# Depthwise convolution taps split anew between four engines

## The reference

```python
def conformer_conv_module(h, w_in, dw, norm_g, norm_b, w_out):
    u = h @ w_in                                  # 2048 -> 4096
    a, g = jnp.split(u, 2, axis=-1)
    u = a * jax.nn.sigmoid(g)
    u = causal_depthwise_conv(u, dw)              # 31 taps per channel
    u = jax.nn.silu(layer_norm(u, norm_g, norm_b))
    return u @ w_out

def causal_depthwise_conv(h, w):                  # out[t] = sum_k w[k] * h[t - 30 + k]
    ...
```

## Time and profile before

| | us |
|---|---|
| median of three runs (2061.01 to 2061.51) | 2061.35 |
| span of the profiled execution | 2059.6 |
| median less span | 1.75 |
| TensorE busy | 2039.1 |
| VectorE busy | 1451.8 |
| ScalarE busy | 981.0 |
| GpSimd busy | 197.6 |

### The profile page before, as it was taken

One profiled execution on the slowest core, in us unless ns is written; L12 is line 12 of the kernel. 1 busy time (PEld: TensorE's weight loads), 2 busy tenths in 40 slices (PEclk: granted clock), 3 DMA queues, 4 the chain that ended last, 5 costly groups with the idle time before them and its releaser, 6 DMA issues.

```text
span 2059.6 us, 36156 instructions
## 1 busy us (share of the span) xinstructions
PE 2039.1 (99%) x11524; PEld 1760.0 (85%) x11524; DVE 1451.8 (70%) x2280; ACT 981.0 (48%) x1295; POOL 197.6 (10%) x123
## 2 busy tenths in 40 slices
PE   9999999999999999999999999999999999999997
PEld 7877888888888888888899988888888888888886
DVE  5477687777677676454699998777777777774545
ACT  4455454444444444343555555544444444444432
POOL 1000000000000000000199920000000000000001
PEclk9999999999999999999999999999999999999999
DMA  7544546656656666555465646565665665676553
GB/s 254 190 129 134 190 150 198 194 177 191 197 183 188 199 203 219 193 193 193 134 189 174 176 154 199 158 198 176 201 193 173 199 193 178 189 256 221 194 192 132
DMA packets 346329, 383.81 MB, mean 186 GB/s; under 512 B 23151, under 2 KB 269471, under 8 KB 345201
## 3 DMA queue, kind: packets, MB, share of 16 engines
q1 hardware_dynamic: 344320, 373.12, 57.4%
q0 software_dynamic: 1360, 7.34, 1.0%
q10 hardware_dynamic: 576, 2.36, 0.3%
HBM read 380.24 MB, written 2.10 MB: 186 GB/s over the span
## 4 chain that ended last, share of the span: by engine, by line
PE 95%; DVE 3%; ACT 1%; issue 0%; DMA 0%; SPq 0%; POOL 0%; POOLq 0%; DVEq 0%; ACTq 0%
PE ps L352 31%; PE ps L348 16%; PE ps L250 11%; PE ps L251 11%; PE ps L252 11%; PE ps L1675 8%; PE ps L265 1%; PE ps L267 1%; PE ps L266 1%; DVE w_lo L218 1%; PE ps L1579 0%; PE ps L1590 0%; PE ps L1606 0%; DVE stats L595 0%; DVE x L589 0%
## 5 line engine op out<-in xcount | busy, mean ns | idle before, releaser
L218 DVE TENSOR_TENSOR w_lo<-raw,w_hi 128x1024 fp32r<-128x1024 f32 x641 | 781.6, 1224 | 489.1 <-ACT w_hi L213 482.4
L213 ACT ACTIVATE w_hi<-raw 128x1024 fp32r<-128x1024 f32 x704 | 743.7, 1059 | 684.6 <-PE ps L252 309.2
L352 PE MATMUL ps<-xT,w_hi 128*128 128x512 f32 x2800 | 960.7, 394 | 0.0
L348 PE MATMUL ps<-xT,w_lo 128*128 128x256 f32 x2800 | 749.7, 277 | 0.0
L352 PEld LDWEIGHTS ps<-xT,w_hi 128*128 128x128 f32 x2800 | 513.2, 188 | 107.2
L348 PEld LDWEIGHTS ps<-xT,w_lo 128*128 128x128 f32 x2800 | 525.9, 188 | 14.9
L250 PE MATMUL ps<-w_hi,hT 128*128 128x512 f32 x828 | 324.2, 392 | 0.2 <-DVE hT L1461 0.2
L252 PE MATMUL ps<-w_hi,hT 128*128 128x512 f32 x828 | 322.4, 389 | 0.0
L251 PE MATMUL ps<-w_lo,hT 128*128 128x512 f32 x828 | 322.3, 389 | 0.0
L1675 PE MATMUL ps<-xT,w_hi 128*128 128x256 f32 x1024 | 191.7, 287 | 1.1 <-DVE xT L709 0.6
L250 PEld LDWEIGHTS ps<-w_hi,hT 128*128 128x128 f32 x828 | 155.4, 188 | 35.2 <-issue 1.4
(11 more groups left out here) (191 smaller groups left out, 1433.7 us busy)
## 6 DMA issues: line engine op xcount, KB each, us to landing
raw<-in_ffn_w_up_dram SPq DMA_DIRECT2D x704, 256.0 KB, 3.2
raw<-in_ffn_w_down_dram SPq DMA_DIRECT2D x352, 256.0 KB, 3.3
raw<-in_conv_w_in_dram SPq DMA_DIRECT2D x128, 256.0 KB, 3.1
raw<-in_attn_wq_dram SPq DMA_DIRECT2D x64, 256.0 KB, 3.3
raw<-in_attn_wo_dram SPq DMA_DIRECT2D x64, 256.0 KB, 3.3
raw<-in_conv_w_out_dram SPq DMA_DIRECT2D x64, 256.0 KB, 3.3
raw<-in_attn_wk_dram SPq DMA_DIRECT2D x16, 256.0 KB, 5.3
raw<-in_attn_wv_dram SPq DMA_DIRECT2D x16, 256.0 KB, 4.2
```

Of the source, the lines that this page charges most:

```text
L213: nc.scalar.activation(w_hi[:, slot, :], raw[:, slot, :], ACT.Copy).then_inc(hi_ready, 1)
L218: v.tensor_tensor(w_lo[:, slot, :], raw[:, slot, :], w_hi[:, slot, :].bitcast(F32), ALU.subtract).then_inc(lo_ready, 1)
L348: nc.tensor.matmul(ps[:, bank, 0:T], wl, xT[:, k, 0:T], start=False, stop=False, skip_group_check=True)
L352: mm = nc.tensor.matmul(ps[:, bank, :], wh, xT[:, k, :], start=(k == 0), stop=(k == KD - 1), skip_group_check=True)
```

## The change

- Tiles 0 to 13: TensorE has no tap, VectorE 27, ScalarE 4 products. GpSimd adds the products in pairs, in one instruction of 2 x 256 columns, and `added` holds two sums. VectorE's first two taps read them as the value to add to (in tile 0 they are added behind tap 18), so an add of VectorE's and the add of TensorE's tap go.
- The gate product of tile `u + 1`, with the statistics behind it, comes behind the 18th tap of tile `u` instead of behind the tile.
- Tile 14: 17 taps on VectorE, 8 products, 6 taps on TensorE (4 between the halves of unit 15, 2 behind it). Tile 15: 9, 8 and 14. What GpSimd adds of the later products goes to `rest`, which VectorE adds (`tile_rest`).
- ScalarE makes tile 15's products between the third and the fourth rounding of `w_out`'s first turn.
- GpSimd makes the low parts of `w_out`'s first turn. The two broadcasts have a bank each, and VectorE's first step waits for them one by one.

```diff
-LAST_PE_TAPS = 16
-MORE_PE_TAPS = 4
-PE_TAPS = 1
-ACT_TAPS = 4
-DVE_TAPS = CW - PE_TAPS - ACT_TAPS
-TILE_STEPS = DVE_TAPS + 1
+ACT_TAPS = [4] * (D // P - 2) + [8, 8]
+PE_TAPS = [0] * (D // P - 2) + [6, 14]
+MID_PE_TAPS = 4
+DVE_TAPS = [CW - a - p for a, p in zip(ACT_TAPS, PE_TAPS)]
+BEFORE_GLU = 18
...
-        diag = at("diag", [P, LAST_PE_TAPS, P], F32, HT_AT)
-        tile_diag = at("tile_diag", [P, 2, MORE_PE_TAPS, P], F32, HT_AT + 12288)
-        products = at("products", [P, ACT_TAPS, T], F32, HT_AT + 16384)
-        added = at("added", [P, T], F32, HT_AT + 16384 + ACT_TAPS * T * 4)
+        diag = at("diag", [P, sum(PE_TAPS), P], F32, HT_AT)
+        products = at("products", [P, max(ACT_TAPS), T], F32, HT_AT + 16384)
+        added = at("added", [P, 2, T], F32, HT_AT + 24576)
+        rest = at("rest", [P, T], F32, HT_AT + 26624)
...
+        def tap_diag(a, i):
+            u = KD - 2 if i < PE_TAPS[KD - 2] else KD - 1
+            j = CW - PE_TAPS[u] + (i if u < KD - 1 else i - PE_TAPS[KD - 2])
+            nc.scalar.activation(diag[:, i], ident[:], ACT.Copy, scale=conv_taps[:, u, j:j + 1]
+                                 ).then_inc(diag_ready, 1)
+        def steps_before(u):
+            return sum(DVE_TAPS[:u]) + (u > 0)
+        def added_used(u):
+            return BEFORE_GLU + 1 if u == 0 else steps_before(u) + 2
...
             if u > 0:
-                a.wait_ge(products_added, 2 * u)
-            for i in range(ACT_TAPS):
-                j = DVE_TAPS + i
+                a.wait_ge(taps, added_used(u - 1))
+            if u == KD - 1:
+                a.wait_ge(products_added, KD + 1)
+            for i in range(ACT_TAPS[u]):
+                j = DVE_TAPS[u] + i
                 nc.scalar.activation(products[:, i], glu[:, u % 2, j:j + T], ACT.Copy,
                                      scale=conv_taps[:, u, j:j + 1]).then_inc(products_made, 1)
...
-                v.wait_ge(pe_taps_done, u - 1)
-                v.wait_ge(products_made, ACT_TAPS * (u - 1))
+                v.wait_ge(products_made, sum(ACT_TAPS[:u - 1]))
...
-        def tile_taps(v, u, n, with_products=False):
...
+        def tile_taps(v, u, between=None):
...
+            o, n, count, last = conv_out[:, u], DVE_TAPS[u], steps_before(u), [0, 0]
+            halves = [ps[:, 4, i * T:(i + 1) * T] for i in range(2)]
             v.wait_ge(glu_done, u + 1)
             if u > 0:
                 v.wait_ge(part_sum, u)
+            if 0 < u < KD - 1:
+                v.wait_ge(products_added, u + 1)
...
+                part, i = halves[j % 2], j % 2
+                tap, src = conv_taps[:, u, j:j + 1], glu[:, u % 2, j:j + T]
+                if u == 0 and j == BEFORE_GLU:
+                    v.wait_ge(products_added, 1)
+                    v.wait_ge(taps, count)
+                    nc.vector.tensor_tensor(ps[:, 4, :], ps[:, 4, :], added[:].rearrange("p a t -> p (a t)"), ALU.add
+                                            ).then_inc(taps, 1)
+                    count += 1
+                    last = [count, count]
+                if between is not None and j == BEFORE_GLU:
+                    between()
+                if j < 2 and u in (0, KD - 1):
                     step = nc.vector.tensor_scalar(part, src, tap, None, ALU.mult)
                 else:
-                    v.wait_ge(taps, base + j - 1)
-                    step = nc.vector.scalar_tensor_tensor(out=o if j == n - 1 else part, in0=src, scalar=tap, in1=part,
+                    if j >= 2:
+                        v.wait_ge(taps, last[i])
+                    step = nc.vector.scalar_tensor_tensor(out=o if j == n - 1 else part, in0=src, scalar=tap,
+                                                          in1=added[:, j] if j < 2 else part,
                                                           op0=ALU.mult, op1=ALU.add)
                 step.then_inc(taps, 1)
-            v.wait_ge(taps, base + n)
-            other = ps[:, 4, n % 2 * T:(n % 2 + 1) * T]
-            nc.vector.tensor_tensor(o, o, other, ALU.add).then_inc(part_sum, 1)
+                count += 1
+                last[i] = count
+            v.wait_ge(taps, count)
+            nc.vector.tensor_tensor(o, o, halves[n % 2], ALU.add).then_inc(part_sum, 1)
+        def tile_rest(v, u):
+            o = conv_out[:, u]
+            v.wait_ge(products_added, KD + 1 if u == KD - 2 else KD + 5)
+            v.wait_ge(part_sum, u + 1)
+            nc.vector.tensor_tensor(o, o, rest[:], ALU.add).then_inc(rest_added, 1)
         def tile_sum(v, u):
             o = conv_out[:, u]
-            v.wait_ge(part_sum, u + 1)
-            v.wait_ge(pe_taps_done, u + 1)
+            v.wait_ge(rest_added, u - KD + 3)
+            v.wait_ge(pe_taps_done, u - KD + 3)
             nc.vector.tensor_tensor(o, o, ps[:, 5 if u < KD - 1 else 1, 0:T], ALU.add).then_inc(tile_done, 1)
...
             with pool.Fori(first + 1, first + KD - 1) as turn:
                 w_in_lows(turn)
-                pool.wait_ge(products_made, turn * ACT_TAPS + (-ACT_TAPS * first))
-                nc.gpsimd.tensor_tensor(products[:, 0:2], products[:, 0:2], products[:, 2:4], ALU.add
-                                        ).then_inc(products_added, 1)
-                pool.wait_ge(products_added, turn * 2 + (-2 * first - 1))
-                nc.gpsimd.tensor_tensor(added[:], products[:, 0], products[:, 1], ALU.add
+                pool.wait_ge(products_made, turn * 4 + (-4 * first))
+                nc.gpsimd.tensor_tensor(added[:], products[:, 0:2], products[:, 2:4], ALU.add
                                         ).then_inc(products_added, 1)
             w_in_lows(first + KD - 1)
+            made = 4 * (KD - 2)
+            pool.wait_ge(products_made, made + 4)
+            nc.gpsimd.tensor_tensor(added[:], products[:, 0:2], products[:, 2:4], ALU.add).then_inc(products_added, 1)
+            pool.wait_ge(products_made, made + 8)
+            nc.gpsimd.tensor_tensor(products[:, 4:6], products[:, 4:6], products[:, 6:8], ALU.add
+                                    ).then_inc(products_added, 1)
+            pool.wait_ge(products_added, KD)
+            nc.gpsimd.tensor_tensor(rest[:], products[:, 4], products[:, 5], ALU.add).then_inc(products_added, 1)
+            w_in_lows(first + KD, (0, 1))
+            pool.wait_ge(products_made, made + 12)
+            nc.gpsimd.tensor_tensor(added[:], products[:, 0:2], products[:, 2:4], ALU.add).then_inc(products_added, 1)
+            pool.wait_ge(products_made, made + 16)
+            nc.gpsimd.tensor_tensor(products[:, 4:6], products[:, 4:6], products[:, 6:8], ALU.add
+                                    ).then_inc(products_added, 1)
+            pool.wait_ge(products_added, KD + 3)
+            nc.gpsimd.tensor_tensor(added[:], added[:], products[:, 4:6], ALU.add).then_inc(products_added, 1)
+            pool.wait_ge(products_added, KD + 4)
+            pool.wait_ge(rest_added, 1)
+            nc.gpsimd.tensor_tensor(rest[:], added[:, 0], added[:, 1], ALU.add).then_inc(products_added, 1)
+            w_in_lows(first + KD, (2, 3))
...
-                tile_diags(a, u)
                 tile_sigmoid(a, u)
-                for i in range(2 * u, min(2 * u + 2, LAST_PE_TAPS)):
-                    j = CW - LAST_PE_TAPS + i
-                    nc.scalar.activation(diag[:, i], ident[:], ACT.Copy, scale=conv_taps[:, KD - 1, j:j + 1]
-                                         ).then_inc(diag_ready, 1)
+                for i in range(2 * u, min(2 * u + 2, sum(PE_TAPS))):
+                    tap_diag(a, i)
                 if u < KD - 1:
                     splits(a, TURN["w_in"] + u + 1, [RING - 1])
+                    tile_products(a, u)
                 if u < KD - 2:
...
-            splits(a, TURN["w_out"])
+            splits(a, TURN["w_out"], range(RING - 1))
+            tile_products(a, KD - 1)
+            splits(a, TURN["w_out"], [RING - 1])
...
-            for u in range(KD - 1):
+            def next_glu(u):
                 tile_glu(v, u)
                 if u % 4 == 2 and u > 2:
                     for tok in range(TT):
                         c_stat(2 * (u // 4 - 1) + tok)
-                if u < KD - 2:
-                    tile_taps(v, u, TILE_STEPS, with_products=True)
-                else:
-                    tile_taps(v, u, CW - PE_TAPS - MORE_PE_TAPS)
-                if u < KD - 2:
-                    tile_sum(v, u)
+            tile_glu(v, 0)
+            for u in range(KD - 2):
+                tile_taps(v, u, lambda: next_glu(u + 1))
+            tile_taps(v, KD - 2)
             tile_glu(v, KD - 1)
+            tile_rest(v, KD - 2)
             tile_sum(v, KD - 2)
-            tile_taps(v, KD - 1, CW - LAST_PE_TAPS)
+            tile_taps(v, KD - 1)
             c_stat(6)
             c_stat(7)
+            tile_rest(v, KD - 1)
             tile_sum(v, KD - 1)
...
-            take_lo(v, TURN["w_out"], 0)
-            v.wait_ge(c_bcast, 1)
...
```

(50 more changed lines are left out.)

46 lines of the change are left out of this document (5 added, 41 removed).

## The result

| | before | after |
|---|---|---|
| median (us), four runs of each | 2061.18 (2060.84 to 2061.51) | 2105.57 (2105.47 to 2105.78) |
| ratio, 95% interval | | 1.0215 (1.0203 to 1.0228) |
| span of the profiled execution | 2059.6 | 2103.8 |
| TensorE busy | 2039.1 | 2047.1 |

The account below looks back on a forecast made before the run. TensorE bounded the kernel, with VectorE next and by a hair the bound after the change; 3.6 (last gate product) + 1.3 (tail) + 0.4 + 0.5 (into w_out), about 5.85 us, off 2061.35 gave 2055.5 us, range 2053.0 to 2063.0.

Parts of the forecast that it names:

- The unknown price: Taps 0 and 1 and the rest sum read two SBUF tensors beside GpSimd: taken as nothing, at most 2.4 us per wait.
- rival 2: In tiles 1 to 13 first taps wait for whole GpSimd instructions, 1.2 to 3.6 us a tile: 2071 to 2102; chance 0.16.
- TensorE's stream: Convolution stage: tiles 0 to 13 lose their TensorE tap, 6.05 us; unit 15's value half ends at 1202.87 instead of 1207.62.
- VectorE's start of tile 1: VectorE waits 2.7 us for GpSimd's sums, then runs free from 1044.6.
- VectorE's tile: A tile without statistics takes VectorE 11.46 us instead of 11.89; last gate product at 1204.3, 3.6 us earlier.
- rival 1: VectorE stays later than worked out through longer steps, stretched taps or late sums: 2059.7 at 0.3 us a tile; chance 0.16.
- The tail: From the last gate product to the last sum: 7.8 us instead of 9.1, 1.3 less.
- Into w_out: The first step's add waits only for the second broadcast, 1221.3 instead of 1221.73: 0.4 us; fewer hT waits: 0.5.
- the hT waits: In w_out TensorE waits twice for VectorE's hT; three fewer VectorE low parts save 0.5 us, bounds 0.2 and 1.0.
- The rest sum: VectorE's add of `rest` at the stage's end reads two SBUF tensors beside GpSimd; no extra time was reckoned.

Follow-up runs that it names:

- experiment 6: Kernel before, with the second tap of tiles 0 to 13 writing its product to SBUF instead of PSUM: 2065.78 us, ratio 1.0023.
- experiment 8: Changed kernel with sums copied to PSUM for the taps, w_out's last two low parts held until the last rest sum, tile 1 begun as tile 0: 2059.51 us.
- experiment 9: As experiment 8, but w_out's last two low parts are VectorE's again, as in the kernel before: 2056.12 us, ratio 0.9976.
- experiment 1: Changed kernel, with taps 0 and 1 of tiles 1 to 14 as plain products that wait for GpSimd's sums without reading them: 2058.74 us, 0.9988.
- experiment 5: Kernel before with only the end of the change (w_out's first low parts by GpSimd, broadcasts in own banks with own waits): 2060.10 us, 0.9995.
- experiment 3: Changed kernel, with each GpSimd low part in the convolution stage made as two instructions of 512 columns: 2084.53 us, ratio 1.0111.

## Why the prediction was wrong

**The step that failed** is "The unknown price", and in it "I take nothing, from the nearest row in kind". The two taps with `added` take 4.2 us in most tiles instead of 0.87, and 9.77 in tile 1. The upper bound, each of the two waiting up to 2.4 us, was the right mechanism and nearly the right size (1.6 and 2.6 us long, so waits of 1.2 and 2.1). My argument from the earlier trace rows proved nothing: those instructions have two SBUF inputs, but no GpSimd add beside them, as the text itself said; it was a row about the instruction, and the question was about its neighbour. The argument against rival 2, that the taps of before read glu from SBUF beside GpSimd with an even spacing, was as weak: they write to PSUM, and experiment 6 shows that a product of the same tap, sent to SBUF, waits. With VectorE as the bound, by the forecast's own working, nothing could absorb the price; rival 2, with its point of decision at 0.45 us per tile, deserved more than 0.16. Its price, 1.2 to 3.6 us a tile, holds the 3.3 measured in most tiles; the time, 2105.57, is above its 2102 because of tile 1 (8.9) and the slow taps at the end.

The page cited in the prediction (the Trainium skill, GPSIMD Engine Reference, Specifications and Key points) names the contention without a size. The forecast did not use another page, the Trainium skill, SBUF — State Buffer, section "Who interferes with whom", which goes further: only the port pair that VectorE shares with GpSimd causes contention, it is an exclusive lock for the whole instruction, an instruction with two SBUF inputs contends with a GpSimd instruction that reads SBUF, so does a `tensor_scalar` in a two-port mode, and one with at most one SBUF input outside those modes does not. The runs here agree with it on which forms wait: 4.14 us for a pair with two inputs (the trace after), 2.55 for a `tensor_scalar` from SBUF to SBUF (experiment 6; that it ran in a two-port mode no run shows), 0.49 for one input to PSUM beside it, 0.44 for the two aggregates with and without a low part beside them (experiments 8 and 9). Tile 1, where three low parts pass before the tap ends, is more than the page says. By that page rival 2 would have been the forecast.

Point by point, the rest:

- *TensorE's stream*: the value half of unit 15 was to end at 1202.87; in experiment 1, where VectorE doesn't hold it up, it does (tile 14's last taps start at 1202.87).
- *VectorE's start of tile 1*: right (1044.43, forecast 1044.6, wait 2.87 for 2.7).
- *VectorE's tile*: 11.46 forecast, 11.54 measured in experiment 1. The step from the sum to the next tile's first tap is 0.51 us (1067.00 to 1067.51), not 0.455; the rest is rounding in the other steps. That the longer step comes from the wait on GpSimd's sums (a third one; the code before has two there, not the one of rival 1) is likely, and no run shows it. 13 tiles make it 1.0 us; the last gate product is at 1205.11 for 1204.3. Rival 1 was right in kind, at a quarter of the size given.
- *The tail*: 7.8 us forecast. In experiment 9 it is 1204.84 to 1212.59, 7.75. In the changed kernel it was 10.4, since TensorE ran the first taps at a granted clock of 0.50 (2.8 us).
- *Into w_out*: 0.4 forecast for the first step; 6.33 became 5.96 after, 5.95 in experiment 9. The 0.5 for the hT waits: 0.8, in the changed kernel (94.07 to 93.25) as in experiments 5 and 9 (93.26). So the bounds of 0.2 and 1.0 held.
- *The rest sum*: the forecast names it among the instructions with two SBUF inputs and prices it at nothing too. It costs 2.1 us in experiment 1, beside a low part that the change itself puts there.

In experiment 9 the median is 5.0 us under that of the kernel before; the forecast had 5.85. Counted from the `memset` at the stage's start (1022.79 before, 1022.30 there), the last gate product comes 2.6 us earlier, not 3.6; the tail gives 1.4 (1.3), the way into w_out 0.4 (0.4), w_out 0.8 (0.5): 5.2. So the terms were nearly right for a kernel in which GpSimd and VectorE don't meet, and the sum is close partly because an error of 1.0 one way meets 0.4 the other. Experiment 1 has the same 2.6 without the easier start of tile 1, so that start gained almost nothing in the end.

**Why 44 us and not 16 or 47.** From experiment 1 to the changed kernel the last gate product moves from 1205.11 to 1251.52, 46.4 us. The pair of tile 1 gives 9.77 - 0.88 = 8.9. In the ten tiles without statistics the pair is 4.14 to 4.23 long, 3.31 over 0.88 on average, 33.1. In two tiles (6 and 10) statistics shift the pair, so that the first tap is issued when a low part is almost over: 0.49 and 2.6, 2.2 each, 4.3. Tile 14's pair comes as GpSimd ends: 0.1. Together 46.4. (Experiment 1's own last gate product is 2.8 us earlier than before; 46.4 - 2.8 is the 43.6 above.) The tiles are alike because the delay is fed back: GpSimd's sums wait for ScalarE's products, these for the gate product, and that for the late taps, so GpSimd starts its four low parts 1.0 us ahead of the next pair every time there (1063.84 and 1064.86, 1078.67 and 1079.66).

**What stays open**: why several GpSimd instructions pass in tile 1 (three, or all halves in experiment 3), while later only the running one does. Two things set tile 1 apart: the tap starts 0.2 us behind the start of a low part, not 1.0, and VectorE has stood idle just before (2.87 us; 3.89 in experiment 3). The first doesn't suffice: the rest sum of experiment 1 starts 0.08 us behind the start of a low part (1212.33), and only that one passes. No run tried this further.

## What to carry to other kernels

Before an operand moves from PSUM to SBUF, list what GpSimd runs at that time, and price the instruction at a whole GpSimd instruction (here 1.6 to 2.6 us for one of 0.48), in every tile if the engine is the bound. A busy share near 100% doesn't show it: look for one group whose mean has grown while its neighbours' has not. If two engines must share the time, an intermediate stop in PSUM by a third engine with slack (0.6 us) costs less than a wait (2060.6 us against 2066.4 here, of which 2.1 are the rest sum's), and a piece of work that is moved to GpSimd "for nothing" has to be checked against everything on the path beside it, two-column instructions too.

## What the hardware showed that I had not expected

- A VectorE instruction that waits in this way ends a little after the GpSimd instruction: 0.29 us for a tap of 256 columns with two SBUF inputs, 0.15 for 256 columns of `tensor_scalar` from SBUF to SBUF (0.34 when free, against 0.49 to PSUM), 0.01 to 0.02 for two columns. That fits work that is done only once GpSimd has ended; the rows don't show it directly.
- The exclusion acts back: the GpSimd instruction behind it takes 2.58 to 2.60 us instead of 2.40 (tile 3), 2.54 behind the rest sum of experiment 1.
- It isn't always the next end of a GpSimd instruction that lets the tap go on: three low parts went by in 7.22 us, and in experiment 3 everything that GpSimd had, in 10.2 us.
- A view of busy time hides it wholly: VectorE is "busy" for 19.75 of 20 us in the window above, as before.
